# Cross output projections: the high parts of the normed rows move from VectorE to ScalarE, the low parts one group later

## The reference

```
x = x + mix
x = x + cross_attn(rmsnorm(x, norm_cross[l]), rmsnorm(mem, norm_mem[l]),
                   xq_w[l], xkv_w[l], xo_w[l], xq_norm[l], xk_norm[l])
x = x + conv_ffn(rmsnorm(x, norm_ffn[l]), ffn_in_w[l], ffn_conv_w[l], ffn_conv_b[l], ffn_out_w[l])
...
def rmsnorm(x, g):
    y = xf * lax.rsqrt(jnp.mean(xf * xf, axis=-1, keepdims=True) + EPS)
    return (y * g.astype(jnp.float32)).astype(x.dtype)
```

## Time and profile before

| | us |
|---|---|
| median of 3 runs | 2550.28 (2548.2 to 2550.37) |
| the profiled execution | 2549.05 |
| its span, first to last instruction | 2547.3 |
| TensorE busy | 2523.1 (99%) |
| VectorE busy | 1755.8 (69%) |
| ScalarE busy | 1145.1 (45%) |
| output projection of the cross attention, layer 0: first residual addition to last square's sum on TensorE | 667.89 to 696.17 |
| the same, layer 1 | 1776.17 to 1802.96 |

### The profile page before, as it was taken

The page is one execution under the profiler, slowest core; times in us unless marked ns, Lnnn a source line. Parts: engine busy times, 40 slices in busy tenths (PEclk is TensorE's granted clock), DMA queues, the critical chain, the costliest instruction groups (busy, mean ns, idle before and its releaser), DMA issues.

```text
span 2547.3 us, 44978 instructions
## 1 busy us (share of the span) xinstructions
PE 2523.1 (99%) x17587; PEld 2279.3 (89%) x17587; DVE 1755.8 (69%) x2485; ACT 1145.1 (45%) x1531; POOL 50.1 (2%) x58
## 2 busy tenths in 40 slices
PE   8999999999999999999999999999999999999999
PEld 7999998999988888888888899999888888888888
DVE  6676676576777756775678767776777667765774
ACT  6444455445444434443444445544444334443443
POOL 2000000010000000000000000010000000000000
PEclk9999999999999999999999999999999999999999
DMA  7444444555455655566565543354556555655654
GB/s 220 126 135 122 133 120 147 166 177 165 147 186 184 199 190 186 184 191 191 179 191 187 179 149 106 118 177 130 161 186 198 190 186 186 192 193 176 198 189 149
DMA packets 428441, 432.38 MB, mean 170 GB/s; under 512 B 13802, under 2 KB 425747, under 8 KB 428304
## 3 DMA queue, kind: packets, MB, share of 16 engines
q1 hardware_dynamic: 423776, 422.46, 53.0%
q0 software_dynamic: 2304, 5.85, 0.7%
q10 hardware_dynamic: 2224, 2.11, 0.3%
HBM read 428.27 MB, written 2.10 MB: 169 GB/s over the span
## 4 chain that ended last, share of the span: by engine, by line
PE 95%; DVE 3%; ACT 1%; issue 0%; DMA 0%; SPq 0%; ACTq 0%; DVEq 0%
PE stream L1760 39%; PE stream L1763 19%; PE stream L1745 10%; PE stream L1746 9%; PE stream L1747 9%; PE bank L1866 1%; PE bank L1727 1%; DVE w_lo L1047 1%; ACT w_hi L580 0%; PE stream L1970 0%; PE bank L2297 0%; PE bank L1931 0%; PE bank L1795 0%; PE bank L2271 0%; PE stream L1973 0%
## 5 line engine op out<-in xcount | busy, mean ns | idle before, releaser
L1047 DVE TENSOR_TENSOR w_lo<-w_raw,w_hi 128x1024 fp32r<-128x1024 f32 x800 | 963.4, 1222 | 483.8 <-ACT w_hi L580 480.4
L580 ACT CAST w_hi<-w_raw 128x1024 fp32r<-128x1024 f32 x800 | 836.8, 1049 | 762.5 <-PE stream L1763 601.9
L1760 PE MATMUL stream<-h,w_hi 128*128 128x512 f32 x2816 | 884.7, 395 | 0.0
L1763 PEld LDWEIGHTS stream<-h,w_lo 128*128 128x128 f32 x2816 | 529.0, 188 | 125.0
L1763 PE MATMUL stream<-h,w_lo 128*128 128x256 f32 x2816 | 553.2, 278 | 0.0
L1745 PE MATMUL stream<-h,w_hi 128*128 128x256 f32 x1536 | 455.0, 296 | 2.5 <-DVE w_lo L1047 2.5
L1760 PE MATMUL stream<-act,w_hi 128*128 128x512 f32 x1408 | 442.8, 396 | 0.0
L1746 PE MATMUL stream<-h,w_hi 128*128 128x256 f32 x1536 | 435.0, 283 | 0.0
L1747 PE MATMUL stream<-h,w_lo 128*128 128x256 f32 x1536 | 434.8, 283 | 0.0
L1760 PEld LDWEIGHTS stream<-h,w_hi 128*128 128x128 f32 x2816 | 428.8, 189 | 0.1
L1763 PEld LDWEIGHTS stream<-act,w_lo 128*128 128x128 f32 x1408 | 264.5, 188 | 62.6
(11 more groups left out here) (424 smaller groups left out, 2009.7 us busy)
## 6 DMA issues: line engine op xcount, KB each, us to landing
w_raw<-in_ffn_in_w SPq DMA_DIRECT2D x352, 512.0 KB, 4.4
w_raw<-in_ffn_out_w SPq DMA_DIRECT2D x176, 512.0 KB, 3.5
w_raw<-in_hyb_in_w SPq DMA_DIRECT2D x96, 512.0 KB, 4.0
w_raw<-in_swa_in_w SPq DMA_DIRECT2D x48, 512.0 KB, 3.5
w_raw<-in_xkv_w SPq DMA_DIRECT2D x32, 512.0 KB, 3.4
w_raw<-in_hyb_out_w SPq DMA_DIRECT2D x32, 512.0 KB, 4.4
w_raw<-in_swa_out_w SPq DMA_DIRECT2D x32, 512.0 KB, 3.6
w_raw<-in_xq_w SPq DMA_DIRECT2D x16, 512.0 KB, 4.1
```

The lines of the kernel that those rows point to most:

```text
L580: nc.scalar.copy(whi[:, k], raw[:, n % NRAW]).then_inc(hi_split, 1)
L1047: v.tensor_tensor(wlo[:, k], raw[:, n % NRAW], whi[:, k].bitcast(F32), ALU.subtract).then_inc(lo_split, 1)
L1760: mm(bank[:, m, :], whi[:, k, kk, w], src[:, kt, :, :], start=(q == 0 and kk == 0), stop=False, skip_group_check=True)
L1763: last = mm(bank[:, m, 0:TOK], wlo[:, k, kk, w], src[:, kt, 0, :], start=False, stop=(q == last_q and kk == len(kts) - 1), skip_group_chec ...
```

## The change

In the eight groups of each layer's cross output projection the two high parts of a group (`h[:, k, 0, :]`) are no longer written by VectorE. ScalarE writes them from `xT` with a per-partition scale, behind its wait for the residual addition and ahead of the square. VectorE writes the low parts of group g - 1 behind the residual addition of group g, and those of group 7 after the loop; it waits for ScalarE's counter `h_hi` to do so. Lines behind the edits move down by 4 (by 15 at the end), so line 1047 of before is 1051 after, 1427 is 1431.

```diff
@@ ScalarE, common(layer)
                     split(XO[layer] + g + AHEAD)
                     if layer == 0 and g == 0:
                         mem_side(1, 16)
+                    act.wait_ge(group_evac, GROUP[XO[layer]] + g + 1)
+                    for k in (2 * g, 2 * g + 1):
+                        last = nc.scalar.activation(h[:, k, 0, :], xT[:, k, :], ACT.Copy, scale=pcol("norm_ffn", KT * layer + k))
+                    last.then_inc(h_hi, 1)
                     residual(S_PHASE[f"xo{layer}"], XO[layer], g, 1)
                 row_rstd(S_PHASE[f"xo{layer}"])
@@ VectorE
+            def x_new_lo(layer, g):
+                dve.wait_ge(h_hi, 24 + 8 * layer + g + 1)
+                for k in (2 * g, 2 * g + 1):
+                    last = v.scalar_tensor_tensor(h[:, k, 1, :], xT[:, k, :], pcol("norm_ffn", KT * layer + k),
+                                                  h[:, k, 0, :].bitcast(F32), ALU.mult, ALU.subtract)
+                last.then_inc(h_ready, 1)
+
             def common(layer):
...
                 for g in range(8):
                     split(XO[layer] + g + AHEAD)
-                    residual(GROUP[XO[layer]] + g, g, XO[layer] + g, "norm_ffn", KT * layer)
+                    residual(GROUP[XO[layer]] + g, g, XO[layer] + g, None, 0)
+                    if g:
+                        x_new_lo(layer, g - 1)
+                x_new_lo(layer, 7)
                 refine_rows(S_PHASE[f"xo{layer}"])
                 ffn(layer)
```

## The result

The changed kernel takes 2564.37 us (median of 4 runs, 2564.17 to 2564.81) against 2549.94 us for the kernel before (4 runs, 2548.2 to 2550.37). The ratio is 1.0061, with a 95% interval of 1.0049 to 1.0073: slower by 0.61%, where 0.46% was forecast. By the medians themselves it is 14.4 us more (0.57%), and 11.8 was forecast. The median lies within the range of 2558 to 2565, near its end; the ratio put on the median of the forecast, 2550.28 x 1.0061 = 2565.8, lies beyond it. So the direction came as forecast and the size was too low. The profiled execution took 2564.81 us, its span is 2562.9 us against 2547.3, that is 15.6 us more.

The account below looks back on a forecast made before the run. TensorE was taken to bound the kernel, held in two stages by a ScalarE-VectorE ring. With p = 0.82 us, 16p - 1.30 = 11.8 us on 2550.28 gave 2562.1 us, slower by 0.46%, range 2558 to 2565.

Parts of the forecast that it names:

- What bounds the stage: Cross output projections: TensorE bounds the kernel, and a chain through ScalarE and VectorE sets how long it waits there.
- The ring: Output projections: square, cast, VectorE's `w_lo`, next addition wait in a circle, 3.46 us a turn, 4.28 after the change.
- What the change removes: VectorE's pair of high-part writes, 0.65 us a group; saving put at 0, since ScalarE's square and cast are nearly level.
- What it adds: Two ScalarE writes a group ahead of the square, delaying what follows by 0.82 us; VectorE's later low parts cost 0.
- p: Delay by ScalarE's new pair to what is behind it in each group: taken as 0.82 us, bounds 0.71 and 0.86.
- The sum: Both output projections: 6.56 us in layer 1 and 5.26 us in layer 0, total 11.8 us.
- last pairs: New ScalarE pair of group 7, ahead of each layer's last square: delays that square by one more 0.82 us.
- the clock's term: Slower TensorE behind long waits at the two stages' ends: nothing in the forecast sum, 5 us in a rival.
- The ring and more: Rival, slower still: TensorE's clock falls for the stage's last 5 us, twice, 5 us more, 2567; 4 in 100.
- The forecast case: Both output projections: 11.8 us slower, 2562.1 us, own range 2559.5 to 2564; 87 in 100.
- TensorE's waits for squares: Both output projections: TensorE's waiting for ScalarE's squares grows from 1.2 to some 13 us in all.
- The chance of the result's sign: Whole kernel: slower 0.90, within 0.2% 0.09, faster 0.01.

Follow-up runs that it names:

- pair_behind_cast: Changed kernel with ScalarE's order in each group made square, cast of the next weights, new pair of high-part writes: 2549.33 us, ratio 1.0000.
- cast_ahead: Changed kernel with ScalarE's cast of the weights one group earlier, ahead of its wait for the addition, then square and pair: 2549.81 us, ratio 1.0000.
- extra_pair: Kernel before, VectorE unchanged, with ScalarE's pair of high-part writes added in each group but written to spare rows: 2564.12 us, ratio 1.0058.
- no_high_parts: Kernel before without VectorE's two high-part writes in these stages, nothing in their place, so computation is missing: 2549.69 us, ratio 1.0002.
- filled_wait: Changed kernel with six filler matmul calls from constants on TensorE ahead of each layer's last sum of squares: 2559.95 us, ratio 1.0042.
- late_last_square: Kernel before with five spare squares on ScalarE ahead of the square of group 7 in both layers: 2557.93 us, ratio 1.0034.
- square_first: Changed kernel with ScalarE's square ahead of the new pair, the pair still ahead of the cast: 2561.33 us, ratio 1.0048.
- one_of_two: Half the change against the kernel before: ScalarE writes one high part of each group, VectorE the other behind the next residual addition: 2557.86 us, ratio 1.0035.
- layer0_only: Kernel before with the change made in layer 0 alone, layer 1 keeping its old order: 2555.57 us, ratio 1.0025.
- cast_ahead_late_sum: Changed kernel with casts one group earlier and TensorE's last sum of squares behind the first feed-forward piece: 2547.20 us, ratio 0.9992.
- late_sum: Changed kernel with TensorE's last sum of squares moved behind its first feed-forward piece: 2554.96 us, ratio 1.0022.

## Why the prediction was right in its mechanism and too low by the clock

**What bounds the stage: right.** The ring through ScalarE's square and cast and VectorE's `w_lo` and addition is the path. It is shown from three sides: pair_behind_cast (same work outside it, turn 3.46 us, no cost), cast_ahead (ring opened, turn 3.74 us, no cost), extra_pair (only ScalarE's part, all of the cost).

**What the change removes, cost 0: right.** no_high_parts, 1.0002. In the changed kernel VectorE's idle time ahead of `w_lo` is 1.64 us; about 1.5 was forecast.

**What it adds, p = 0.82 us: 0.81.** The 32 new ACTIVATE have a median of 504 ns, and the pair holds the square back by 0.81. The bounds were 0.71 and 0.86, and the choice near the upper one, by source and kind of operand, was right. By the formula of the Trainium skill ("ScalarE: Activation LUTs", What ACT_TABLE_LOAD costs) it was 0.80 us; the trace agrees.

**The sum, 11.8 us: 11.45 measured** for the ring and its last pairs (10.6 by the medians of filled_wait, where the clock stayed up). A turn is 4.26 us where I added up 4.28: the square stands 0.52 us ahead of the cast in place of 0.54, the rest is the pair. Layer 1 from its first addition to its last sum of squares is 6.35 us longer (6.6 forecast). Layer 0's last sum starts at 698.63, and with the 1.47 us by which the stage began earlier in this execution that is 700.10; 700.3 was forecast.

**The step that failed** is the clock's term. The sum put it at nothing, and the range with it; it stood only in the case "The ring and more": "If the clock fell to its lower level for as much as the stage's last 5 us, twice, it would be 5 us more: 2567", given 4 in 100. I had the wait (one of some 4 us at each stage's end; 3.12 measured, twice) and nearly the price (5; 4.4 by the medians, 5.6 in the profiled execution), and argued the case away with one row: TensorE busy for 13.01 of 16.70 us at a clock of 1.00. That row was the wrong witness. The longest pause that the trace has in that stretch is 1.20 us, and it says nothing of one of three. It wasn't even a safe witness for its own kind: in 6 of the 12 experiments the clock fell in that same stretch. The forecast case should have carried the clock's term, 11.8 + 5 = 16.8 us, or the two cases should have shared the chance, with a range up to 2567. That the median still lies within the range is luck: its upper end was to allow for something mis-sized in the turns, not for the clock.

The Trainium skill ("TensorE: Matmul & The Clock Gate", Why this matters for your kernels) advises against long idle gaps between bursts of matmuls, since the throughput drops behind them. The trace agrees: the granted clock is 0.50 behind waits of 3.12 us. That rule spoke against this change, and it wasn't weighed.

**TensorE's waits for squares, forecast as some 13 us, are 9.0 us** in 13 waits, the longest 3.1. The forecast counted everything that a turn grows by as waiting. The rows count part of it as busy time, at a clock of 1.00: TensorE's timeline shows a wait of 0.26 us in a turn that is 4.26 - 3.74 = 0.52 us longer than its own. Behind a wait the sum of squares lasts 1.13 us in place of 1.03, and it starts when the matmul before it has ended, where it otherwise starts before that. For the 11 waits more than before that is about 2.9 us, an estimate from these rows (filled_wait shows 2.6 us), and it is most of the gap.

**The chance of the result's sign** was right: of all orders tried, those that left the pair on the ring are slower, and those that took it off are level. None is shown to be faster than the kernel before.

## What to carry to other kernels

Where two engines work in order and each waits for the other once a turn, follow the chain through one full turn: an instruction that is put between the release and what the ring needs next costs its whole length each turn from where the ring is the slower path, however idle its engine is on the mean; the same instruction behind it cost nothing here, and the cast one turn earlier opened the ring. When an edit lengthens a wait of the bounding engine, price two things, the wait and TensorE's clock behind it, and take as the witness for the clock a row with a single wait of that length. If TensorE must wait, give it work there, best the next stage's first piece (9.4 us here), else even useless matmuls (4.4 us).

## What the runs showed of the hardware that was not expected

**Idle TensorE time costs beyond itself.** At the ends of the two stages the granted clock fell to 0.50 behind every wait for the last square of 2.44 to 3.27 us (11 of 11 such waits in six profiled kernels: the changed one, late_last_square, extra_pair, square_first, one_of_two, layer0_only), and behind none of 0.34 to 1.71 us. Between these nothing was tried, and what the chip looks at isn't shown by it.

**A fall doesn't have one price.** Worked out from the stretches, it cost 2.7 and 2.9 us in the changed kernel, 2.8 and 1.4 us in extra_pair (the same waits of 3.12 us), 1.6 and 1.4 us in late_last_square, and 1.5 to 1.6 us at the five places of square_first, one_of_two and layer0_only (less 1.6 us where the stretch also holds the fall told of next). The price goes with the length. Added up over windows of 0.5 us as above, the granted clock was at 0.50 for 6.8 us at the three dear places and for 3.4 us at the eight others; no other length came up. So a fall costs about half of the time at 0.50, less what of that time lies in the wait itself. In square_first the four matmuls of layer 0's last sum lasted 1.22 us, not 2.07: behind the same wait the fall came later. What decides between the two lengths stays open.

**The clock also falls where the waits are shorter, and then not in every kernel.** Behind the attention's last steps of layer 1, TensorE's waits are alike in the two kernels below, and the clock is not. First the kernel before, then no_high_parts, columns as in the earlier trace rows:

```profile
1764.00:1768.00 4.00, 2.07 (x11) 1.33 (x9) 3.81 (x11) 2.88 (x9) 0.00 (x0) 1.00 0.00 0
1768.00:1772.00 4.00, 3.79 (x29) 3.69 (x30) 0.92 (x3) 1.53 (x2) 0.00 (x0) 1.00 0.01 2
```

```profile
1764.00:1768.00 4.00, 2.00 (x11) 1.26 (x9) 3.83 (x11) 2.88 (x9) 0.00 (x0) 1.00 0.00 0
1768.00:1772.00 4.00, 3.86 (x19) 3.68 (x20) 0.09 (x1) 1.53 (x2) 0.00 (x0) 0.60 0.00 2
```

The code of this stretch is the same in both. Such a fall makes the stretch between the layers 1.6 us longer (1084.1 in place of 1082.5 us). It is there in the profiled executions of no_high_parts, pair_behind_cast, one_of_two, layer0_only, cast_ahead and cast_ahead_late_sum. The time at 0.50 is again 3.4 us in each of the six. The runs without a profile point the same way: of the 33 of the kernel before beside late_sum, the 8 with a mean granted clock of 1.000 have a median of 2547.5 us, the 25 with 0.999 one of 2549.5. In filled_wait 4 of 5 runs have 1.000, of the kernel before beside it 2 of 16, which may be why its ring costs 10.6 us by the medians and 11.45 by the additions; no run tests that. One execution of a kernel of this kind is therefore uncertain by some 2 us that no instruction of it explains. Whoever works out a change from two profiled executions must look at the clock outside of the changed stage as well.
